# A two-layer hybrid encoder on one core: softmaxed attention weights turned by VectorE block transposes and a trip through DRAM

## The reference, cut to what matters

```python
def sink_softmax(scores, sink, mask=None):
    s = scores.astype(jnp.float32)
    if mask is not None:
        s = jnp.where(mask, s, -jnp.inf)
    sk = jnp.broadcast_to(sink[:, :, None, None].astype(jnp.float32), s.shape[:-1] + (1,))
    return jax.nn.softmax(jnp.concatenate([s, sk], axis=-1), axis=-1)[..., :-1]
...
    pr = sink_softmax(jnp.einsum('bcqkgd,bcskd->bckgqs', qr, kb), sink, valid)
    orr = jnp.einsum('bckgqs,bcskd->bcqkgd', pr.astype(v.dtype), vb).reshape(B, nc * CHUNK, SWA_HEADS * HEAD_DIM)
```

## Time and profile before

| | |
|---|---|
| median of 3 runs | 3056.57 us (3056.52 to 3057.87) |
| the profiled execution's own time | 3056.32 us |
| its span, first to last instruction | 3054.4 us |
| PE busy | 3011.8 us, 99% |
| VectorE busy | 1529.4 us, 50% |
| ScalarE busy | 939.6 us, 31% |
| data moved | 760.19 MB, mean 249 GB/s |
| granted TensorE clock | 0.999 of full speed |

### The profile page before, as it was taken

One profiled execution on the slowest core, in us unless ns is written; L12 is line 12 of the kernel. 1 busy time (PEld: TensorE's weight loads), 2 busy tenths in 40 slices (PEclk: granted clock), 3 DMA queues, 4 the chain that ended last, 5 costly groups with the idle time before them and its releaser, 6 DMA issues.

```text
span 3054.4 us, 64343 instructions
## 1 busy us (share of the span) xinstructions
PE 3011.8 (99%) x27180; PEld 2759.9 (90%) x27180; DVE 1529.4 (50%) x3672; ACT 939.6 (31%) x2381; POOL 216.8 (7%) x319
## 2 busy tenths in 40 slices
PE   8999999999999999999999999999999999999998
PEld 7788778889898899989989899999999999999998
DVE  4345552355633455336554366544566255663562
ACT  3324440134421343124341144303343043421320
POOL 0111010011101110010010101000000000000000
PEclk9999999999999999999999999999999999999999
DMA  7577477788978989888797898986768857787887
GB/s 256 170 205 213 118 208 218 220 237 283 311 236 263 280 273 320 242 259 272 238 313 210 264 276 261 295 284 196 260 205 268 290 178 249 210 267 253 301 302 248
DMA packets 227116, 760.19 MB, mean 249 GB/s; under 512 B 25088, under 2 KB 44672, under 8 KB 226576
## 3 DMA queue, kind: packets, MB, share of 16 engines
q1 hardware_dynamic: 189328, 620.80, 61.6%
q0 software_dynamic: 37504, 135.28, 18.0%
HBM read 744.33 MB, written 136.31 MB: 288 GB/s over the span
## 4 chain that ended last, share of the span: by engine, by line
PE 92%; DMA 3%; DVE 3%; ACT 2%; issue 0%; SPq 0%; ACTq 0%; DVEq 0%
PE psum L1853 29%; PE psum L1306 27%; PE psum L1876 10%; PE psum L1912 8%; PE psum L1443 7%; DMA slots<-in_weights 2%; PE psum L1300 1%; PE psum L1322 1%; PE psum L1621 1%; PE psum L1646 1%; DMA slots<-wsum 1%; PE psum L1633 1%; PE psum L1572 1%; PE psum L1694 1%; PE psum L1803 1%
## 5 line engine op out<-in xcount | busy, mean ns | idle before, releaser
L1306 PE MATMUL psum<-hT,slots 128*128 128x256 f32 (+1 forms) x2880 | 658.9, 387 | 2.8 <-ACT hT L874 2.1
L1306 PEld LDWEIGHTS psum<-hT,slots 128*128 128x128 f32 x2880 | 541.6, 190 | 97.0 <-issue 5.5
L1853 PE MATMUL psum<-tsum,slots 128*128 128x128 f32 (+1 forms) x4928 | 608.0, 277 | 11.6 <-ACT raw L1223 4.9
L1853 PEld LDWEIGHTS psum<-tsum,slots 128*128 128x128 f32 x4928 | 573.1, 191 | 28.6 <-issue 20.2
L1853 PE MATMUL psum<-hT,slots 128*128 128x128 f32 (+1 forms) x3696 | 453.7, 276 | 6.9 <-DMA slots<-in_weights 3.9
L1853 PEld LDWEIGHTS psum<-hT,slots 128*128 128x128 f32 x3696 | 432.6, 192 | 10.1 <-DMA slots<-in_weights 4.9
L1876 PE MATMUL psum<-gT,slots 128*128 128x256 f32 (+1 forms) x1408 | 309.9, 383 | 0.0
L1876 PEld LDWEIGHTS psum<-gT,slots 128*128 128x128 f32 x1408 | 267.1, 190 | 40.9
L1306 PE MATMUL psum<-mixT,slots 128*128 128x256 f32 (+2 forms) x1024 | 226.4, 381 | 1.1 <-DVE hT L2030 1.1
L1306 PEld LDWEIGHTS psum<-mixT,slots 128*128 128x128 f32 x1024 | 194.3, 190 | 29.7 <-issue 1.5
L2030 DVE SCALAR_TENSOR_TENSOR hT<-hT,psum 128x256 f32<-128x256 f32 (+2 forms) x96 | 40.5, 423 | 348.3 <-PE psum L1876 249.7
(11 more groups left out here) (326 smaller groups left out, 3526.6 us busy)
## 6 DMA issues: line engine op xcount, KB each, us to landing
slots<-in_weights SPq DMA_DIRECT2D x667, 512.0 KB, 4.6
slots<-wsum SPq DMA_DIRECT2D x308, 512.0 KB, 4.5
wsum<-in_weights POOLq DMA_DIRECT2D x132, 512.0 KB, 6.7
slots<-wsumi SPq DMA_DIRECT2D x64, 512.0 KB, 4.4
slots<-wsumd SPq DMA_DIRECT2D x64, 512.0 KB, 4.5
wsum<-wsum POOLq DMA_DIRECT2D x44, 512.0 KB, 7.9
wsumi<-in_weights POOLq DMA_DIRECT2D x24, 512.0 KB, 7.5
wsumd<-in_weights POOLq DMA_DIRECT2D x24, 512.0 KB, 9.3
```

The source lines that it names most:

```text
L1306: ins = mm(psum[:, i % 2, :n], lhsT, rhs, start=k == 0, stop=k == len(pairs) - 1)
L1853: ins = mm(dst[:, e * n:(e + 1) * n], w[:, (4 * e + k) * P:(4 * e + k + 1) * P], moving[s][k], start=s in (0, 1, 5) and e == 0 and k == 0, ...
```

## The change

For the 12 full tiles of chunks 2 to 7 (`weights_by_blocks`), PE's 8 transposes and ScalarE's two copies go. Instead VectorE transposes the scaled weights in 32x32 blocks (two instructions), back into the score buffer, now 1024 columns wide. SyncE writes that buffer to DRAM (`weights_to_dram`, the put, 512 KB) and reads it back (`weights_by_keys`, four gets of 128 KB in two pairs) so that the blocks land with keys on partitions. The put is issued after the fourth dense step behind the lane step of VectorE's transposes, the gets six and seven dense steps later. The values are multiplied nine lane steps after the scores instead of four, so a tile takes 10 lane steps. The 28-block row pitch of `PR` (224 columns instead of 208) lets the transposes read whole blocks. The 16-token tiles and chunks 0 and 1 are as before. The reserve for GpSimd's DMA descriptors is halved to make room.

```diff
+def weights_by_blocks(u, j):
+    return u > 1 and j > 0
+
...
+VALUES_STEP, PUT_AFTER, GET_AFTER = 9, 4, 10
...
+def lane_block(u, step):
+
+    return AT[u - 1, f"us{step // 3}_{2 * (step % 3) + 1}"]
+
+
+def weight_turns():
+
+    out = {}
+    for nth, (u, j) in enumerate(ALL_TILES):
+        if weights_by_blocks(u, j):
+            i, nt, k = [t for t, _, _ in tiles_of(u)].index(j), len(tiles_of(u)), tiles_where(weights_by_blocks, nth)
+            start = 3 * nt + 3 + (5 if nt == 3 else 0) + (VALUES_STEP + 1) * (i - (nt == 3))
+            out[lane_block(u, start + 1) + PUT_AFTER] = ("put", k)
+            for half in range(2):
+                out[min(lane_block(u, start + 1) + GET_AFTER, AT[u - 1, f"us{GROUPS - 1}_5"]) + half] = ("get", k, half)
+    return out
...
-        SC = sb("SC", 4 * WIN)[:, :].rearrange("p (h s) -> p h s", h=4)
+        sc = sb("SC", 1024)
+        SC = sc[:, 0:4 * WIN].rearrange("p (h s) -> p h s", h=4)
...
-        PR = prpt[:, 0:4 * WIN].rearrange("p (h s) -> p h s", h=4)
+        PR = prpt[:, 0:28 * BLOCK].rearrange("p (h s) -> p h s", h=4)
+        PC = sc[:, 0:1024].rearrange("p (q m c) -> p q m c", q=4, m=2)
+        PB = prpt[:, 1024:2048].rearrange("p (b m c) -> p b m c", b=4, m=2)
+        pdram = nc.dram_tensor("pdram", (P, 1024), F32, kind="Internal").ap()
...
+            def weights_to_dram(nth):
+
+                sp.wait_ge(S["p_cut"], nth + 1)
+                if nth:
+                    sp.wait_ge(S["p_in"], 64 * nth)
+                sp.dma_start(pdram, sc[:, 0:1024]).then_inc(S["p_out"], 16)
+
+            def weights_by_keys(nth, half):
+
+                sp.wait_ge(S["p_out"], 16 * (nth + 1))
+                source = pdram.rearrange("(b s) (q c) -> q s b c", b=4, q=4)
+                for q in (2 * half, 2 * half + 1):
+                    sp.dma_start(PB[BLOCK * q:BLOCK * (q + 1)].rearrange("p b m c -> p b (m c)"), source[q]).then_inc(S["p_in"], 16)
...
+                    if name0[:2] == "us" and AT[u0, name0] in turns:
+                        what, *which_turn = turns[AT[u0, name0]]
+                        (weights_to_dram if what == "put" else weights_by_keys)(*which_turn)
...
-                    a.wait_ge(S["a_pt"], nth + 1)
+                    if weights_by_blocks(u, j):
+                        for _ in range(VALUES_STEP - 3):
+                            yield
+                        a.wait_ge(S["a_oT"], nth + 1)
+                        for g in range(2):
+                            ins = act(mixT[:, 2 + g, off:off + P].rearrange("p (b s) -> p b s", b=4),
+                                      bank(BX)[:, 0:2 * P].rearrange("p (b g s) -> p g b s", b=4, g=2)[:, g], ACT.Copy)
+                        ins.then_inc(S["a_mix"], 1)
+                        yield
+                        continue
...
-                    pe.wait_ge(S["a_pn"], nth + 1)
+                    if weights_by_blocks(u, j):
+                        for _ in range(VALUES_STEP - 3):
+                            yield
+                        pe.wait_ge(S["p_in"], 64 * (tiles_where(weights_by_blocks, nth) + 1))
+                        for m in range(2):
+                            rows_m = min(w - P * m, P)
+                            for kv in range(2):
+                                ins = mm(bank(BX)[HD * kv:HD * kv + HD, 0:2 * P].rearrange("p (b c) -> p b c", b=4),
+                                         Vw[:rows_m, b, m, HD * kv:HD * kv + HD],
+                                         PB[:rows_m, :, m, 2 * BLOCK * kv:2 * BLOCK * (kv + 1)], start=m == 0, stop=m == 1)
+                        ins.then_inc(S["a_oT"], 1)
+                        yield
+                        continue
...
-                    tt(PR[:n_, :, :w], PR[:n_, :, :w], rden[:n_, :, None].broadcast_to([n_, 4, w]),
-                       ALU.mult).then_inc(S["a_pn"], 1)
+                    ins = tt(PR[:n_, :, :w], PR[:n_, :, :w], rden[:n_, :, None].broadcast_to([n_, 4, w]), ALU.mult)
+                    if weights_by_blocks(u, j):
+                        after(step(ins))
+                        for m in range(2):
+                            ins = v.transpose(PC[:, 0:4 - m, m].rearrange("p q (h s) -> p q h s", h=4),
+                                              PR[:, :, P * m:P * m + P - BLOCK * m].rearrange("p h (q s) -> p q h s", s=BLOCK))
+                        ins.then_inc(S["p_cut"], 1)
+                        for _ in range(VALUES_STEP - 4):
+                            yield
+                    else:
+                        ins.then_inc(S["a_pn"], 1)
...
-    nc = bacc.Bacc("TRN2", target_bir_lowering=False, num_devices=1, dynamic_dma_scratch_size=2048)
+    nc = bacc.Bacc("TRN2", target_bir_lowering=False, num_devices=1, dynamic_dma_scratch_size=1024)
```

More of the change, by code:

```diff
@@ L116 @@
 DN_BLOCKS = 3
+ALL_TILES = [(u, j) for u in range(NU) for j, _, _ in tiles_of(u)]
 DN_SLOTS = 8 * DN_BLOCKS
@@ L124, with keys_by_blocks, tiles_where, tiles_not @@
 SWA_PART = ["sq0", "sq1", "sk", "sv"]
+def keys_by_blocks(u, j):
+    return u > 0 and j > 0
+def weights_by_blocks(u, j):
+    return u > 1 and j > 0
+def tiles_where(test, nth):
+    return sum(test(*tile) for tile in ALL_TILES[:nth])
+def tiles_not(test, nth):
+    return nth - tiles_where(test, nth)
 def input_part(u):
@@ L515, in build @@
             "r_tr", "r_kc", "r_vc", "r_sc", "r_sm", "r_state", "r_o", "r_oc", "r_ssq", "r_sd", "r_mix",
-            "a_kept", "a_window", "a_vt", "a_vtc", "a_sc", "a_scm", "a_max", "a_exp", "a_es", "a_pn", "a_pt", "a_ptc",
+            "a_kept", "a_window", "a_vt", "a_vtc", "a_sc", "a_scm", "a_max", "a_exp", "a_es", "a_pn", "p_cut", "p_out", "p_in", "a_pt", "a_ptc",
             "a_oT", "a_mix",
@@ L636, in _ @@
             sp.dma_start(ln_in_sb[:, :], ln_in).then_inc(S["in_first"], 16)
+            turns = weight_turns()
             for i, (l, which, u, name, q) in enumerate(USES):
@@ L695, in _ @@
             g.memset(PCp, 1.0).then_inc(S["init"], 1)
+            g.memset(sc[:, 28 * BLOCK:1024], 0.0).then_inc(S["init"], 1)
             g.wait_ge(S["in_con"], 16)
@@ L1180, in side @@
                     yield
-                    a.wait_ge(S["a_pt"], nth + 1)
+                    if weights_by_blocks(u, j):
[8 more added lines that the diff above has]
+                        continue
+                    a.wait_ge(S["a_pt"], tiles_not(weights_by_blocks, nth) + 1)
                     for m in range(2 if j else 1):
@@ L1791, in side @@
                     yield
-                    pe.wait_ge(S["a_pn"], nth + 1)
+                    if weights_by_blocks(u, j):
[11 more added lines that the diff above has]
+                        continue
+                    pe.wait_ge(S["a_pn"], tiles_not(weights_by_blocks, nth) + 1)
                     for m in range(2 if j else 1):
@@ L1798, in side @@
                     yield
-                    pe.wait_ge(S["a_ptc"], nth + 1)
+                    pe.wait_ge(S["a_ptc"], tiles_not(weights_by_blocks, nth) + 1)
                     for m in range(2 if j else 1):
@@ L2774, in end_step @@
                     scale_tile(0, 2)
-            v.wait_ge(S["init"], 5)
+            v.wait_ge(S["init"], 6)
             rest(*(input_tile(j) for j in range(3)))
```

## The result

The changed kernel takes 3068.43 us (median of 5 runs, 3065.07 to 3073.34), the kernel before 3056.55 us beside it (5 runs, 3053.42 to 3057.87): 1.0043 times as long, 95% interval 1.0032 to 1.0054. I had said 3046.4 us and faster. It is slower by 0.43%, which is 13 us by the ratio and 12 by the medians, and past the end of my range (3060).

What follows compares the result with a forecast made beforehand. PE was taken to bound the kernel, busy 3011.8 of 3054.4 us. 3056.3 - 11.6 (transposes) - 3.3 (exponentials) + 4.8 (transfers) = 3046.2, stated as 3046.4 us; range 3038 to 3060, the forecast's own 3043 to 3050.

Steps and rivals of the forecast that it cites:

- transposes gone: On PE, 8 transposes fewer in each of 12 tiles, 0.97 us a tile: -11.6 us.
- second tile's later exponentials: Exponentials move to lane step 20, where ScalarE can start sooner; five PE waits of 0.66 us go: -3.3 us.
- put and gets: DMA transfers of 3.2 to 4.8 us a tile, mostly hidden from PE: +4.8 us.
- VectorE's new work: Block transposes of 1.1 us a tile, 13 us in all, on an engine idle half the span: cost nothing.
- So I charge one transfer of 1.6 us in full in each of three stretches: Among the attention stretches of chunks 2 to 5, PE sees one transfer in each of three: +4.8 us.
- a ring that holds 2.6 us in reserve: Weight blocks, issued 7.1 us before use, land after 4.5 us; the spare 2.6 us fits a 1.6 us put.
- The second, slower: Rival: transfers of eight tiles in the stretches with GpSimd's sums fully exposed at double price, 38 us: 3080 us; chance 0.10.
- its milder case: Milder version of the slower rival: 20 to 28 us of transfers exposed, giving 3062 to 3069 us.
- the second gain: PE's five waits of 0.66 us for ScalarE vanish as the second tile's exponentials move later: -3.3 us, the least certain gain.
- The first rival: DMA takes most back: half of eight tiles' transfers exposed, 13 to 19 us, giving 3054 to 3061 us; chance 0.13.
- The third: Rival: VectorE's late convolutions delay ScalarE; bank waits stay or grow at lane step 20: 3049.5 to 3061 us; chance 0.13.
- The fourth, all hidden: Rival: PE sees none of the DMA transfers, giving 3041 us; chance 0.14.

Runs made afterwards that it cites:

- e3: The kernel before, transposes kept on PE, with each full tile of chunks 2 to 7 stretched to 10 lane steps: 3058.73 us, 1.0005.
- e1: The changed kernel without puts and gets; PE reads what `prpt` holds and waits for VectorE's transposes instead: 3045.93 us, 0.9964 of the kernel before.
- e2: The kernel before with only the reserve for GpSimd's DMA descriptors halved: 3053.34 us, 0.9992.
- e12: The changed kernel with a tile's four gets behind four dense steps, one each, not two and two: 3067.47 us, 1.0031 of the kernel before.
- e4: The changed kernel with the new path in chunks 6 and 7 alone: 3050.11 us, 0.998 of the kernel before.
- e5: The changed kernel with the new path in chunks 2 to 5 alone: 3070.16 us, 1.0038 of the kernel before.
- e8: The changed kernel without GpSimd's weight sums for the second layer's input and down projections: 3035.53 us, 0.9938 of the kernel before.
- e9: The kernel before without GpSimd's weight sums for the second layer's input and down projections: 3043.48 us, 0.9962.
- e13: The kernel before without those GpSimd sums (e9), with full tiles of chunks 2 to 7 stretched to 10 lane steps (e3): 3044.68 us, 0.9965.
- e14: The kernel before with only chunk 4's two full tiles stretched to 10 lane steps: 3060.38 us, 1.0014.
- e15: The kernel before with the full tiles of chunks 3, 5, 6 and 7 stretched to 10 lane steps: 3054.98 us, 0.9999.
- e7: The changed kernel with all 48 gets but 11 of the 12 puts left out: 3059.24 us, 1.001 of the kernel before.
- e6: The changed kernel with the puts kept and the 48 gets left out: 3054.32 us, 0.9996 of the kernel before.

## Why the prediction was wrong

By its own steps, in the ratios above:

| part | forecast us | measured us |
|---|---|---|
| transposes gone | -11.6 | -12.5, good to 5 (e3 to e1; holds the last two rows as well) |
| second tile's later exponentials | -3.3 | +1.5, interval -1 to +4 (e3) |
| put and gets | +4.8 | +22.5 to +24 (e1 to after) |
| VectorE's new work | 0 | one wait of 0.76 in chunk 4, within the first row |
| descriptor reserve | 0 | -2.4 [-5, 0] (e2), within the first row |

**The step that failed is the sentence "So I charge one transfer of 1.6 us in full in each of three stretches".** What a tile's transfers take of the engines' time stays within my 3.2 to 4.8 us for all that the runs show, but they don't pin it: the kernels with GpSimd's sums and 620.80 MB in SyncE's queue spent between 1832 us (e2) and 1881 us (before) on them, and the two with 633.39 MB 1899 and 1892 us (after and e12), which is 1 to 5.5 us a tile. What PE saw is measured: 22.5 us. If nothing of it is seen in chunks 6 and 7, as e4 suggests, it is 2.8 us for each of the eight tiles of chunks 2 to 5, most of the price, where I had charged 0.6 us (4.8 over 8). By e5, with two thirds of the -12.5 and the stretch's +1.5 taken off, it is 2.3 to 2.6. PE's waits for blocks grew against e1 in the stretches of all four chunks (by 1.3, 2.8, 3.9 and 3.7 us), and chunks 6 and 7 have none.

Two readings led me there.

First, I took the DMA share over 72 and 120 us, and in these means 0.85 and 0.93 look like slack. They lie over saturated and free pieces, as the pieces above show: 1.01 and 0.81, 0.97 and 0.71. My reading of e8 and e9 is this: where all engines' time is asked for, a transfer moves every later block by its own length until a free piece comes, and a ring that holds 2.6 us in reserve doesn't absorb it.

Second, I read "only 10.2 us of waiting for blocks in the whole trace" as evidence of slack. It says only that demand and supply were balanced so far. Waits of 1.75 and 2.23 us were the signs that the reserve was used up. One of the prediction's own signs of being wrong came true: a get took 4.5 us to land. The put took 5.1 us, where I had taken 2.6 from the two output transfers of the earlier trace rows; its gets came late enough that nothing waited for it.

A third part is only argued, and no run shows it. The sums are tied to dense steps 11 to 50. If PE goes through these faster, since transposes are gone (or lane work is moved out, as the stretch does), the same transfers fall into less time, and what PE saved returns as waits for blocks. The pair that bears on it doesn't decide: the stretch over all chunks costs 1.5 us with the sums (e3) and 1 us without (e13). The 4 us of e14 have no partner without the sums.

**Rivals.** The second, slower, is what happened, in its milder case: 20 to 28 us exposed, 3062 to 3069. I had its mechanism, its place and its price, and gave it 0.10. That 3068.4 lies in its range is part luck, though: with both gains kept, 22.5 us would have given 3064, and the rest is the second gain, which didn't come. The first rival named the same mechanism at half the exposure and 0.13. The third did not come at lane step 20: the trace has no wait for ScalarE there in the five chunks with a second tile at that step. But VectorE was late in two other places. One is chunk 3's input tiles, which I had not followed: a chain that begins behind a lane moves with the lane's end. The other is the first full tile of chunk 4, where the block transposes (1559.07 to 1560.24 us) and the group's convolutions stand ahead of `rwkv`'s part (L2556), and PE waits for it:

```profile
1562.85 0.34 PE L1702 MATMUL psum<-wset 64*64 64x64 f32 x8 [0.76 <-DVE wset L2556]
```

The same wait stands in the traces of e1 and e8, and not in e3's, which has the stretch without the block transposes. The fourth, all hidden, fits only chunks 6 and 7. A put that SyncE holds back for VectorE, and values that wait for `prpt` from DRAM, show in none of the changed kernel's waits.

**What the second gain became.** The five waits of 0.66 us did go, one of the same length came in chunk 4, and no time came of it. That is the second term that failed: it was put at -3.3 us, and e3 measures the whole stretch at -1 to +4. The half-clock pieces explain part. The changed kernel's trace has three (from 881.2, 1591.3 and 1922.4 us), each about 3.4 us long and worth about 1.7 us, against one before; e3 has one, at 881.9 us, which takes 1.7 of its 3.3 us. Where e15's saving is stays open: its trace has fewer waits of the first kind and its time is that of the kernel before.

## What to carry to other kernels

Before adding a transfer, take the DMA share of both queues together over tens of us and not over a stage (40 and 80 us showed here what 120 hid). Where it is 1.00, charge most of the engine time of the transfer, puts and small-piece gets, to the bound engine. Few waits in a trace show that supply is in balance, not that there is slack. Try such a change first in the stages where the share is well below 1: here the same edit gained 6 us in chunks 6 and 7 and lost about twice that in the others.

## What the runs showed of the hardware

- **Half clock after short gaps, but not after all.** PE's granted clock fell to about half for some 3.4 us right behind idle gaps of 2.2 us, and in the changed kernel of 2.86, 3.19 and 3.42 us; no gap of up to 1.84 us in these two traces was followed by it. Other traces show full clock behind gaps as long: 2.18 us in e3 (1583.00 us), 2.86 in e7 (1941.37), 2.87 in e12 (881.14) and 2.96 in e5 (1580.64). The same wait for chunk 3's input tile is followed by half clock in the changed kernel and in e3, and by full clock in e8 and e12. So a wait of 3 us can cost nearer 5, and doesn't always.
- **Block transposes on VectorE.** 711 ns for 128x512 and 536 ns for 128x384, where 1236 ns for 128x1024, scaled by columns, gives 618 and 464: 15% more for either.
- **Gets in 1 KB pieces.** They cost PE 13.3 us against the puts' 8.4 for the same bytes by the medians (e7, e6, e1), with intervals that touch. Without the sums (e8) the put landed in 3.8 us and a get in 4.1, with them in 5.1 and 4.5 (medians).
- **Spread.** With the same program the runs of the kernel before lie up to 12 us apart (3049.89 to 3061.89 over 21 of them in the last batch), far more than the 1.4 us of the first three.
